# A two-layer decoder trunk: input projection dealt into a latent block of 328 columns and two groups' values as 512, gate with features on partitions, and x, w_in and the vectors laid out ahead

## The chip, the cores and the metric

The kernel runs on one core of a Trainium2 chip. The metric is the device time in microseconds (us) of one execution, as the median of several runs. The profile is one further execution, recorded by the hardware profiler.

## What is computed

All arithmetic is float32. `x` is 256 tokens by 1024 features, and there are two layers. Of the reference, what matters here:

```python
cond = silu(c)
for l in range(2):
    sh1, sc1, g1, sh2, sc2, g2 = split(cond @ w_ada[l] + b_ada[l], 6)
    h = rms_norm(x, norm1_gain[l]) * (1.0 + sc1) + sh1
    proj = h @ w_in[l]
    (qa, ka, va, qb, kb, vb, qc, kc, vc, fc, gc,
     qlat, kvlat, kidx, widx) = split(proj)   # nine of 256, then 4, 256, 128, 128, 64, 4
    ...                                       # four head groups: differential, block, forgetting, indexed
    o_c = forgetting_attention(qc, kc, vc, fc + f_bias[l]) * sigmoid(gc)
    q_lat, kv_lat = rms_norm(qlat), rms_norm(kvlat)
    ...                                       # q, k, v and the index scores of the fourth group from these
    x = x + g1 * (concat(o_a, o_b, o_c, o_d) @ w_out[l])
    h = rms_norm(x, norm2_gain[l]) * (1.0 + sc2) + sh2
    x = x + g2 * conv_glu_ffn(h, w_ffn_up[l], ffn_conv_w[l], ffn_conv_b[l], w_ffn_down[l])
return rms_norm(x, final_gain)
```

The input projection has 2888 columns: 9 x 256 for q, k and v of three groups (a, b, c), and 584 more: forget logits (4), gate (256), latents (128 + 128), index key (64), index weights (4).

## The kernel before

**Units.** Every large weight is used in units of 1 MB (128 partitions x 2048 floats). SP loads a unit into one of three buffers `raw`; ACT copies it, rounded, to `w_hi` (`split_hi`, L1437); DVE subtracts to get `w_lo` (`split_lo`, L1693); PE then computes three products per tile, hi x hi, hi x lo and lo x hi (`product3`, L979 to L981). Activations are split in the same way into `act_hi` (ACT, L1463) and `act_lo` (DVE, L1708). A buffer is loaded again when its `split_lo` three units back is done; `w_hi` is written again when PE has used that unit.

**The twelve units of the input projection** are `IN_UNITS`: unit 0 has the last 72 columns (index key, index weights and the rest of the latents) with features on partitions, which PE then transposes back (`narrow`, L1224); unit 1 has 256 and unit 2 the first 256 of the 584 columns (forget logits and nearly all of the gate); units 3 to 11 are q, k, v of the three groups, 256 columns each. For a unit PE goes over eight tiles of 128 input features (k) and two halves, which makes 48 matmuls of 256 moving columns (24 for unit 0). In q and k units the weights stand still and the 256 tokens move, so that features come out on partitions; in the others the activations stand still and the weight columns move, so that tokens come out on partitions. PE writes units alternately to PSUM banks 0 and 1, and may write a bank again when ACT has copied the unit before out of it (`evac`, L1513 to L1519, counted by the semaphore `in_read`).

**The gate** comes out with tokens on partitions, goes through a tanh on ACT and a scaling on DVE in the step `forget` (L1547, L1842), and is transposed in the middle of the attention (`gate_turn`: four PE transposes at L1339, one ACT copy at L1601), because the third group's output has features on partitions.

**Order of work.** `layer_schedule(l)` writes one list of steps; each engine goes through the list and issues its own part of every step, in that order. After the first units come the latents (norm, transposes L1231 and L1236, up-projections L1247 and L1251), the index scores (L1262), the forget sums, and then `maps()`, called thirteen times. Each call issues the scores of two heads on PE (L1188, L1190), the bias and minimum on DVE (L1889, L1891), the exponentials on ACT (L1578), and the transposes of earlier probabilities (L1299); halves of the remaining units stand between the calls and fill PE while DVE and ACT work. The step `choose` (top 64 of the index scores, L1863, L1864) is spread over DVE between them.

**Setup, before layer 0.** SP issues c, x, then `w_ada` units ("direct", 1 MB each, eight of them for the first shift and scale) mixed with the vectors as rows and the first units of `w_in`. PE transposes x (16 matmuls, L1124) and DVE copies it to `xT` (L1769); PE transposes the vectors too (L1114). PE multiplies the eight units with `cond` (L992, 16 matmuls each, two records to one matmul), two of them giving one quarter of shift and scale, and waits with dummy products (`keep_busy`, L1137). A quarter goes to `mod` through a transpose and an add on DVE (L1736, L1738). Shift (units 0 to 3) is loaded before scale (units 4 to 7) in each half:

```python
SETUP_COLUMNS = (0, SETUP_ADA // 2, 2, SETUP_ADA // 2 + 2)   # pairs: shift, scale, shift, scale
```

Of the kernel before, what the change touches and what calls it, by code (L numbers as in the profile page):

```python
# [22 lines left out]
P = 128  # L23
# [9 lines left out]
UC = 256  # L33
# [7 lines left out]
IN_COLS = C_FC + HEADS + GROUP + 2 * P + HEAD + HEADS  # L41
TAIL = IN_COLS - C_FC
T_GC, T_LAT = HEADS, HEADS + GROUP
T_KIDX = T_LAT + 2 * P
# [43 lines left out]
V_BADA, V_N1, V_N2, V_CB = 0, 48, 56, 64  # L88
V_W0, V_W1 = 128, 128 + 2 * FT
V_W2 = 256  # L90
VROWS = [64 + 2 * FT, 4 * FT, 2 * FT]
# [49 lines left out]
SETUP_COLUMNS = (0, SETUP_ADA // 2, 2, SETUP_ADA // 2 + 2)  # L141
# [25 lines left out]
def layer_schedule(l):  # L167
# [61 lines left out]
    if l == 0:  # L229
        s += [("unit", 0, 4, KT), ("evac", 0), ("split_hi", 3), ("unit", 1, 4, KT), ("evac", 1), ("split_lo", 3),  # L230
              ("unit", 2, 0, 4), ("narrow", 0), ("unit", 2, 4, KT), ("evac", 2), ("latents_norm", 0),
              ("split_hi", 4), ("split_lo", 4), ("unit", 3, 0, KT), ("evac", 3), ("latents", 0), ("lambda", 0),
              ("forget", 0), ("split_hi", 5), ("split_lo", 5)]
    else:
        for k in range(KT):
            s += [("unit", 0, k, k + 1), ("unit", 1, k, k + 1)]
        s += [("evac", 0), ("evac", 1), ("narrow", 0)]
        s += [("split_hi", 3), ("latents_norm", 0), ("split_lo", 3), ("unit", 2, 0, 4)]
# [8 lines left out]
    def first_half(i):  # L247
        s.append(("unit", i, 0, KT // 2))

    def second_half(i):  # L250
        s.extend([("unit", i, KT // 2, KT), ("evac", i)])
# [58 lines left out]
    s.append(("gate_turn", 0))  # L310
# [43 lines left out]
def trunk(nc, x, c, ada_units, b_ada, norm1_gain, w_in, f_bias, diff_lambda, diff_subln_gain, w_dq_up,  # L354
          w_didx_q, w_dkv_up, w_out, t5_table, norm2_gain, w_ffn_up, ffn_conv_w, ffn_conv_b,
          w_ffn_down, final_gain, buckets, out):
# [6 lines left out]
    with ExitStack() as ctx:  # L363
# [3 lines left out]
        def sem(name):  # L367
# [17 lines left out]
        tail = sb("tail", [P, TT, TAIL])  # L385
# [5 lines left out]
        vec = sb("vec", [P, DEPTH, 384])  # L391
# [29 lines left out]
        c_rows = sb("c_rows", [KT, P])  # L421
# [13 lines left out]
        narrow = work[0:NARROW, 768:768 + SEQ]  # L435
# [10 lines left out]
        gate_c = tail[:, :, T_GC:T_GC + GROUP]  # L446

        x_tok = heads_out[:, :, :, :].rearrange("p g t n -> p (g t n)").rearrange("p (t n) -> p t n", t=TT)
        rows_in = v_sb[:, 0:3, :, :].rearrange("p g t n -> p (g t n)")[:, 0:DEPTH * 384].rearrange(
            "p (l r n) -> p l r n", l=DEPTH, r=3)  # L450
# [15 lines left out]
        rows_sem = [sem("rows_early"), sem("rows_late")]  # L466
# [5 lines left out]
        c_turned = sem("c_turned")  # L472
        table_in = sem("table_in")
        diag_up = sem("diag_up")
        vec_turned = sem("vec_turned")
        x_turned = sem("x_turned")
# [32 lines left out]
        narrow_turned = sem("narrow_turned")  # L509
        narrow_read = sem("narrow_read")  # L510
# [29 lines left out]
        gate_turned = sem("gate_turned")  # L540
# [7 lines left out]
        gate_exp = sem("gate_exp")  # L548
# [29 lines left out]
        def vector_rows(l, t):  # L578

            return VROWS[t]  # L580

# [14 lines left out]
        def unit_bank(l, i):  # L596
            if (l, i) == (0, 2):
                return bank[2]
            return bank[i % 2 if i < NI else i - NI]
# [11 lines left out]
        def unit_width(i):  # L611
            return IN_UNITS[i][2] if i < NI else UC

# [28 lines left out]

        def unit_shape(i):

            return KT * unit_width(i)

# [28 lines left out]
        for st, i in [e[:2] for e in schedules[0]]:  # L675
            if st == "probs":
                turn_order.append(("probs", i))
            elif st == "turn" and i not in SIDE:
                turn_order += [("turn", i, 0)]
            elif st == "gate_turn":  # L680
                turn_order.append(("gate_turn", 0))
# [1405 lines left out]
```

## Time and profile before

| | |
|---|---|
| median of three runs | 727.2 us (727.04 to 727.21) |
| the profiled execution, its own time | 725.33 us |
| span of its profile | 723.6 us |
| PE busy | 699.5 us of the span |
| DVE, ACT, POOL busy | 504.2, 398.1, 121.9 us |
| read from HBM | 156.81 MB |

The span runs from the first to the last instruction; the execution's own time is 1.7 us longer. Matmuls overlap in the pipeline, so the duration of one is longer than its distance from the next, and an engine counted as busy can hide short waits. Stretches of the run: setup to about 38 us, layer 0's attention to about 160, its MLP to about 375, then the same for layer 1.

### The profile page before, as it was taken

Reading aid. Unit: us, or ns where it says so; the run is one execution under the profiler, and the core shown is the slowest. Engines: PE = TensorE matmul, PEld = TensorE weight load, DVE = VectorE, ACT = ScalarE, POOL = GpSimd, SP = SyncE. Lnnn points to the kernel's source line nnn. Section 1 sums busy time; section 2 is a strip of 40 time slices with the busy share of each in tenths; the row PEclk is TensorE's granted clock in tenths of the full one; section 3 lists DMA queues with packets and bytes.
Section 4 is the critical chain, followed back from the end, with each engine's and each line's share of the span. In section 5 each row is a group of like instructions: output and inputs, shape, how many; then the busy total and the mean of one; then the engine's idle time right before and its main releaser. Section 6 shows DMA issues by size and latency. Waiting matters only on the chain.

```text
span 723.6 us, 15426 instructions
## 1 busy us (share of the span) xinstructions
PE 699.5 (97%) x6461; PEld 660.3 (91%) x6461; DVE 504.2 (70%) x905; ACT 398.1 (55%) x644; POOL 121.9 (17%) x96
## 2 busy tenths in 40 slices
PE   6999999999999999999999999979999999999995
PEld 5898989899999999999999998869999999999993
DVE  2464788736888879887757568973687666666666
ACT  3258756735756464646445775573475555544552
POOL 2001003004044635363010010210400000000002
PEclk9999999999999999999999999999999999999998
DMA  9989998465386767687744875556526567555511
GB/s 320 382 221 249 395 341 323 178 234 175 118 291 233 260 207 256 210 291 254 286 131 137 299 265 191 187 221 234 175 83 215 164 211 249 187 175 175 183 50 58
DMA packets 98151, 159.43 MB, mean 220 GB/s; under 512 B 6035, under 2 KB 85028, under 8 KB 91940
## 3 DMA queue, kind: packets, MB, share of 16 engines
q1 hardware_dynamic: 98084, 158.46, 63.9%
q8 instruction: 51, 0.84, 0.5%
q14 instruction: 16, 0.13, 0.1%
HBM read 156.81 MB, written 1.64 MB: 219 GB/s over the span
## 4 chain that ended last, share of the span: by engine, by line
PE 78%; DVE 9%; ACT 6%; issue 3%; DMA 2%; SPq 1%; POOL 0%; DVEq 0%; POOLq 0%; ACTq 0%
PE bank L979 23%; PE bank L980 22%; PE bank L981 22%; PE bank L992 3%; DVE w_lo L1693 2%; ACT work L1578 2%; DMA direct<-in_w_ada 2%; DVE score L1864 1%; ACT w_hi L1437 1%; DVE top L1863 1%; PE bank L1025 1%; PE bank L1299 1%; SPq L747 1%; PE bank L1330 1%; DVE work L1889 1%
## 5 line engine op out<-in xcount | busy, mean ns | idle before, releaser
L1693 DVE TENSOR_TENSOR w_lo<-raw,w_hi 128x2048 fp32r<-128x2048 f32 (+1 forms) x97 | 238.4, 2458 | 95.2 <-ACT w_hi L1437 95.0
L979 PE MATMUL bank<-act_hi,w_hi 128*128 128x256 f32 (+1 forms) x1024 | 293.1, 286 | 0.3 <-DVE act_lo L1708 0.2
L980 PE MATMUL bank<-act_lo,w_hi 128*128 128x256 f32 (+1 forms) x1024 | 289.6, 283 | 0.0
L981 PE MATMUL bank<-act_hi,w_lo 128*128 128x256 f32 (+1 forms) x1024 | 289.6, 283 | 0.0
L1437 ACT ACTIVATE w_hi<-raw 128x2048 fp32r<-128x2048 f32 (+1 forms) x97 | 183.0, 1888 | 135.3 <-PE bank L981 133.2
L979 PEld LDWEIGHTS bank<-act_hi,w_hi 128*128 128x128 f32 (+1 forms) x1024 | 195.5, 191 | 4.3 <-issue 3.1
L980 PEld LDWEIGHTS bank<-act_lo,w_hi 128*128 128x128 f32 (+1 forms) x1024 | 195.6, 191 | 0.4
L981 PEld LDWEIGHTS bank<-act_hi,w_lo 128*128 128x128 f32 (+1 forms) x1024 | 195.5, 191 | 0.0
L1985 DVE SCALAR_TENSOR_TENSOR work<-bank,vec,work 128x254 f32<-128x254 f32 (+1 forms) x176 | 76.5, 476 | 11.2 <-ACT work L1637 9.6
L979 PE MATMUL bank<-mlp_hi,w_hi 128*128 128x256 f32 x192 | 54.7, 285 | 0.0
L980 PE MATMUL bank<-mlp_lo,w_hi 128*128 128x256 f32 x192 | 54.3, 283 | 0.0
L981 PE MATMUL bank<-mlp_hi,w_lo 128*128 128x256 f32 x192 | 54.3, 283 | 0.0
L1578 ACT ACTIVATE work<-work,low 128x128 f32<-128x128 f32 x80 | 35.6, 446 | 33.5 <-DVE low L1889 33.2
L1637 ACT ACTIVATE work<-bank,vec 128x256 f32<-128x256 f32 x88 | 44.3, 553 | 17.5 <-PE bank L981 17.4
L979 PE MATMUL bank<-w_hi,act_hi 128*128 128x256 f32 (+1 forms) x168 | 49.5, 294 | 0.1
L980 PE MATMUL bank<-w_lo,act_hi 128*128 128x256 f32 (+1 forms) x168 | 48.3, 288 | 0.0
L981 PE MATMUL bank<-w_hi,act_lo 128*128 128x256 f32 (+1 forms) x168 | 48.3, 287 | 0.0
L881 POOL TENSOR_TENSOR direct<-direct 128x1024 f32<-128x1024 f32 (+1 forms) x16 | 42.5, 2657 | 24.7 <-ACT direct L1455 23.8
L992 PE MATMUL bank<-direct,cond 128*32 128x128 f32 x1280 | 41.1, 277 | 0.6 <-DMA direct<-in_w_ada 0.6
L992 PEld LDWEIGHTS bank<-direct,cond 128*32 128x32 f32 x1280 | 33.7, 111 | 4.0 <-issue 1.0
L979 PEld LDWEIGHTS bank<-mlp_hi,w_hi 128*128 128x128 f32 x192 | 36.8, 192 | 0.3 <-issue 0.3
L980 PEld LDWEIGHTS bank<-mlp_lo,w_hi 128*128 128x128 f32 x192 | 36.8, 192 | 0.0
(214 smaller groups left out, 949.0 us busy)
## 6 DMA issues: line engine op xcount, KB each, us to landing
direct<-in_w_ada SPq DMA_DIRECT2D x48, 1024.0 KB, 8.9
raw<-in_w_ffn_up SPq DMA_DIRECT2D x44, 1024.0 KB, 5.2
raw<-in_w_in SPq DMA_DIRECT2D x22, 1024.0 KB, 6.7
raw<-in_w_ffn_down SPq DMA_DIRECT2D x22, 1024.0 KB, 4.9
raw<-in_w_out SPq DMA_DIRECT2D x8, 1024.0 KB, 4.9
bias<-toeplitz SPq DMA_DIRECT2D x4, 384.0 KB, 11.3
heads_out<-in_x SPq DMA_DIRECT2D x1, 1024.0 KB, 5.0
out<-heads_out SPq DMA_DIRECT2D x4, 256.0 KB, 2.2
```

The costliest lines, as they stand in the source:

```text
L747: sp.dma_start(dst, src).then_inc(raw_in[n % RAW], 16)
L881: nc.gpsimd.tensor_tensor(w[:, 0:m], w[:, 0:m], w[:, m:2 * m], ALU.add).then_inc(ada_added, 1)
L979: pe.matmul(dst, lh, rh, start=first, stop=False, skip_group_check=check)
L980: pe.matmul(dst, lh, rl, start=False, stop=False, skip_group_check=check)
L981: return pe.matmul(dst, ll, rh, start=False, stop=last, skip_group_check=check)
L992: mm = pe.matmul(pair_bank(l, u)[32 * g:32 * g + 32, 0:P], cond[:, 4 * half + k, :], w[:, k, g, :], start=(half == 0 and k == 0), stop=(ha ...
L1025: mm = pe.matmul(means[:, t, :], wide[:, k, t * P:(t + 1) * P], mean_w[:, 0:1].to_broadcast([P, MEAN_COLS]), start=(k == early_tiles(n) an ...
L1437: nc.scalar.activation(w_hi[n % RAW][:, 0:KT * width], raw[n % RAW][:, 0:KT * width], ACT.Copy).then_inc(hi_done, 1)
L1578: nc.scalar.activation(part, part, ACT.Exp, bias=low[:, i % 3, t:t + 1], scale=-1.0, accum_out=rsum[:, sum_slot(i)[0], t, sum_slot(i)[1]:s ...
L1637: nc.scalar.activation(conv[:, which, f, :], bank[which][:, f * SEQ:(f + 1) * SEQ], ACT.Identity, scale=vec[:, l, V_W2 + ch:V_W2 + ch + 1] ...
L1693: nc.vector.tensor_tensor(w_lo[n % RAW][:, s], raw[n % RAW][:, s], w_hi[n % RAW][:, s].bitcast(F32), ALU.subtract).then_inc(lo_done, 1)
L1985: ins = nc.vector.scalar_tensor_tensor(dst, bank[which][:, f * SEQ:(f + 1) * SEQ - lag], vec[:, l, tap + ch:tap + ch + 1], dst, ALU.mult, ...
```

## The change

The 584 columns are dealt anew. A latent block of 328 columns (latents, index key, index weights, forget logits) has tokens on partitions and takes banks 0 and 1, one for each half of the tokens. It comes in two units: tiles 0 to 5 (128 x 1968 floats) and tiles 6 and 7 (128 x 656). The 256 gate columns become a unit of their own with features on partitions, the eleventh, copied out through the tanh into `gate_T`; `gate_turn` and `narrow` go. The values of groups a and b become one block of 512 columns, again in two units of four tiles each, and banks 0 and 1 hold one half of the tokens each; both are copied out after the second unit. The host lays out `w_in`, `x`, `c` and the vectors so that every partition reads one contiguous run. PE's transposes of x, c and the vectors, and DVE's copies, go. In the setup scale is loaded before shift, and the loads and products are in another order.

```diff
-IN_UNITS = [("tail", 512, TAIL - 512), ("tail", 256, 256), ("tail", 0, 256)]
-NARROW = TAIL - 512
-IN_UNITS += [(what, g, UC) for g in range(3) for what in "qkv"]
+IN_UNITS = [("lat", 0, LAT, 0, 6), ("lat", 0, LAT, 6, KT), ("q", 0, UC, 0, KT), ("k", 0, UC, 0, KT),
+            ("vv", 0, 2 * UC, 0, KT // 2), ("vv", 0, 2 * UC, KT // 2, KT), ("q", 1, UC, 0, KT), ("k", 1, UC, 0, KT),
+            ("q", 2, UC, 0, KT), ("k", 2, UC, 0, KT), ("gate", 2, UC, 0, KT), ("v", 2, UC, 0, KT)]
+READ_BY = {("k", 0): 4, ("k", 1): 8, ("k", 2): 10, ("v", 0): 6, ("v", 1): 6, ("v", 2): 12}
...
-SETUP_COLUMNS = (0, SETUP_ADA // 2, 2, SETUP_ADA // 2 + 2)
+SETUP_COLUMNS = (SETUP_ADA // 2, 0, SETUP_ADA // 2 + 2, 2)
...
+            s.append(("tokens", i, 1))
+            if i == 5:
+                s.extend([("evac", 4), ("evac", 5)])
...
-                    src = w_in[l].rearrange("(k p) n -> p k n", p=P)[:, :, c0:c0 + width]
-                    dst = dst[:, 0:KT * width].rearrange("p (k n) -> p k n", k=KT)
+                    src = in_units[l, i, :, 0:unit_cols(i)]
+                    dst = dst[:, 0:unit_cols(i)]
...
+                for k, t in order:
+                    if wait_act is not None:
+                        pe.wait_ge(act_lo_ready, wait_act + k + 1)
+                    s = slice(t * P, (t + 1) * P)
+                    mm = product3(bank[t][:, 0:cols], (act_hi[:, k, s], act_lo[:, k, s]),
+                                  (wh[:, k - first, :], wl[:, k - first, :]), k == 0, k == KT - 1)
+                    if k == KT - 1 and t == 0:
+                        mm.then_inc(tokens_half, 1)
...
+                    elif st == "tokens":
+
+                        pe.wait_ge(in_read, NI * l + (4 if e[2] else 1))
+                        first = IN_UNITS[i][3]
+                        mm = wide_product(l, i, [(k, e[2]) for k in range(first, first + KT // 2)])
...
+                        if i in (0, 4):
+                            act.wait_ge(tokens_half, 2 * l + (2 if i else 1))
+                        else:
+                            act.wait_ge(unit_used, unit_no(l, i) + 1)
...
+                        elif kind == "vv":
+                            nc.scalar.activation(v_sb[:, 0:2, i - 4, :], bank[i - 4][:, :].rearrange("p (g n) -> p g n", g=2),
+                                                 ACT.Copy).then_inc(in_read, 1)
+                        elif kind == "gate":
+                            nc.scalar.activation(gate_T[:, :, :], src, ACT.Tanh, scale=0.5).then_inc(in_read, 1)
...
+            take_mod(0, 6)
+            first_low(4, 6)
+            split_lo(1, unit_cols(1))
+            first_low(6, KT)
+            front_part(1)
```

In layer 1 unit 2 (now q of group a) is written to bank 7, in layer 0 to bank 2 as unit 2 was before. The first call of `maps()` still stands between the two halves of unit 5.

**SP, the loads of the setup** (in_w_ada: the eight units; raw: the units of `w_in`; the four rows after the first two ada units before are the vectors as rows). Before:

```order
L774 DMA heads_out<-in_x 128x2x1024
L727 DMA direct<-in_w_ada 128x2048 x2
L717 DMA v_sb<-in_b_ada 48x2x128
L717 DMA v_sb<-in_norm_gain 8x2x128 x2
L717 DMA v_sb<-in_ffn_conv_b 44x2x128
L727 DMA direct<-in_w_ada 128x2048
L747 DMA raw<-in_w_in 128x8x72
L747 DMA raw<-in_w_in 128x8x256
L727 DMA direct<-in_w_ada 128x2048 x5
```

And now:

```order
L758 DMA xT<-in_x 128x2048
L708 DMA direct<-in_w_ada 128x2048 x2
L761 DMA vec<-in_vectors 128x480
L708 DMA direct<-in_w_ada 128x2048
L726 DMA raw<-in_w_in 128x1968
L708 DMA direct<-in_w_ada 128x2048
L765 DMA tab<-in_t_table 32x12
L766 DMA own_bias<-in_buckets 33x384
L708 DMA direct<-in_w_ada 128x2048 x2
L755 DMA raw<-in_w_in 128x1024
L708 DMA direct<-in_w_ada 128x2048 x2
L726 DMA raw<-in_w_in 128x656
```

The second unit of `w_in` stood ahead of the last five ada units; now the first one, larger, stands ahead of five, and half of unit 2 ahead of the last two.

**PE, the start of the setup**, before and then now:

```order
L1120 MATMUL bank<-ident,c_rows 128x8
L1124 MATMUL bank<-ident,heads_out 128x128 x16
L992 MATMUL bank<-direct,cond 32x128 x16
L1025 MATMUL bank<-mean_w,work 128x32 x10
L992 MATMUL bank<-direct,cond 32x128 x16
L1048 MATMUL bank<-ident,root 128x128 x2
L1114 MATMUL bank<-ident,v_sb 128x108 x2
L992 MATMUL bank<-direct,cond 32x128 x16
L1137 MATMUL bank<-ident 128x128 x20
```

```order
L1114 MATMUL bank<-ident 128x128 x13
L971 MATMUL bank<-direct,cond 32x128 x16
L1004 MATMUL bank<-mean_w,work 128x32 x10
L971 MATMUL bank<-direct,cond 32x128 x16
L1027 MATMUL bank<-ident,root 128x128 x2
L971 MATMUL bank<-direct,cond 32x128 x16
L1114 MATMUL bank<-ident 128x128 x24
L1127 MATMUL bank<-own_bias,tab 12x384
L971 MATMUL bank<-direct,cond 32x128 x32
```

The transposes are gone, dummy products stand in their place, and the table product (L1127) has moved ahead of the fourth ada unit.

**ACT, around the first `maps()`** (work,rsum<-work,low are the exponentials, v_sb<-bank the copy of values out of PSUM), with what each row waits for. Before:

```order
L1578 ACTIVATE work,rsum<-work,low 128x128 [waits low_ready]
L1578 ACTIVATE work,rsum<-work,low 128x256 [waits low_ready]
L1517 ACTIVATE v_sb<-bank 128x512 [waits unit_used]
L1437 ACTIVATE w_hi<-raw 128x2048 [waits unit_used,raw_in2]
L1578 ACTIVATE work,rsum<-work,low 128x128 [waits low_ready]
```

And now:

```order
L1540 ACTIVATE work,rsum<-work,low 128x128 [waits low_ready]
L1540 ACTIVATE work,rsum<-work,low 128x256 [waits low_ready]
L1476 ACTIVATE v_sb<-bank 128x2x256 [waits tokens_half]
L1476 ACTIVATE v_sb<-bank 128x2x256 [waits unit_used]
L1400 ACTIVATE w_hi<-raw 128x2048 [waits unit_used,raw_in2]
L1540 ACTIVATE work,rsum<-work,low 128x128 [waits low_ready]
```

Before, the copy of unit 4 stood ahead of the exponentials; now both copies of values stand behind them, and PE's next unit needs the first (it writes bank 0).

## Rows read from the trace of the kernel before

**Rows 1.** The page: the span; busy time and share of each engine.

```profile
span 723.6 us, 15426 instructions
...
PE 699.5 (97%) x6461; PEld 660.3 (91%) x6461; DVE 504.2 (70%) x905; ACT 398.1 (55%) x644; POOL 121.9 (17%) x96
```

**Rows 2.** PE waits, layer 0: line, released by, us in total, times, longest.

```profile
PE bank L1188 <- ACT qkT L1519: 0.7, 2, 0.6
PE bank L1299 <- DVE work L1925: 0.7, 1, 0.7
```

**Rows 3.** The same view, layer 1.

```profile
PE bank L1188 <- ACT qkT L1519: 2.2, 2, 1.7
PE bank L1330 <- DVE work L1900: 0.9, 1, 0.9
...
PE bank L1349 <- DVE work L1900: 0.6, 1, 0.6
```

**Rows 4.** Timeline of PE, equal matmuls in a row: start us, us (256 columns).

```profile
300.05 0.28 PE L980 MATMUL bank<-act_lo,w_hi 128*128 128x256 f32 x1
...
308.45 0.28 PE L981 MATMUL bank<-act_hi,w_lo 128*128 128x256 f32 x1
```

**Rows 5.** The same view, matmuls of 512 columns.

```profile
602.20 0.39 PE L980 MATMUL bank<-w_lo,mlp_hi 128*128 128x512 f32 x1
...
606.51 0.39 PE L981 MATMUL bank<-w_hi,mlp_lo 128*128 128x512 f32 x1
```

**Rows 6.** Windows: stretch, length, busy us of each engine, PEclk, DMA share, GB/s.

```profile
0.00:10.00 10.00, 3.93 (x21) 3.53 (x25) 2.14 (x4) 3.14 (x7) 2.37 (x15) 1.00 0.77 294
10.00:20.00 10.00, 9.97 (x151) 9.05 (x151) 2.09 (x5) 3.58 (x7) 2.13 (x3) 1.00 1.08 365
20.00:30.00 10.00, 9.18 (x144) 8.16 (x146) 6.35 (x12) 2.60 (x5) 0.00 (x0) 1.00 1.01 420
```

**Rows 7.** Timeline of PE: setup, latents, first index product, transposes of the gate.

```profile
22.12 1.08 PE L992 MATMUL bank<-direct,cond 128*32 128x128 f32 x32 [0.62 <-DMA direct<-in_w_ada]
...
25.83 0.31 PE L979 MATMUL bank<-act_hi,w_hi 128*72 128x256 f32 x1 [0.21 <-DVE act_lo L1708]
...
58.08 2.76 PE L1247 MATMUL bank<-heads_out,direct 128*128 128x256 f32 x12
...
65.21 0.50 PE L1262 MATMUL bank<-kiT,qiT 64*128 64x128 f32 x4 [0.65 <-ACT v_sb L1542]
...
119.71 0.60 PE L1339 MATMUL bank<-ident,tail 128*128 128x128 f32 x4
```

**Rows 8.** ACT groups, by form: busy us, mean ns.

```profile
L1437 ACT ACTIVATE w_hi<-raw 128x2048 fp32r<-128x2048 f32 x95 | 181.6, 1913 | 135.3 <-PE bank L981 133.2 <-DMA raw<-in_w_in 2.0
...
L1463 ACT ACTIVATE act_hi<-work,mod 128x256 fp32r<-128x256 f32 x32 | 15.7, 507 | 33.8 <-DVE work L1712 33.8
...
L1480 ACT ACTIVATE w_hi<-raw 128x1024 fp32r<-128x1024 f32 x1 | 1.0, 1042 | 0.0
```

**Rows 9.** DVE groups, by form.

```profile
L1693 DVE TENSOR_TENSOR w_lo<-raw,w_hi 128x2048 fp32r<-128x2048 f32 x95 | 236.9, 2493 | 95.1 <-ACT w_hi L1437 95.0
...
L1708 DVE SCALAR_TENSOR_TENSOR act_lo<-work,mod,act_hi 128x256 fp32r<-128x256 f32 x32 | 15.3, 479 | 1.7 <-ACT act_hi L1463 1.7
```

**Rows 10.** Timeline of PE, around the first maps() of layer 0.

```profile
73.48 0.49 PE L1188 MATMUL bank<-qkT 32*128 32x128 f32 x4
...
74.34 0.39 PE L979 MATMUL bank<-w_hi,act_hi 128*128 128x256 f32 x1
```

**Rows 11.** Timeline of ACT, the same stretch.

```profile
79.22 0.57 ACT L1517 ACTIVATE v_sb<-bank 128x512 f32<-128x512 f32 x1
```

**Rows 12.** Timeline of PE, layer 1, end of unit 1 and start of unit 2.

```profile
390.15 0.36 PE L979 MATMUL bank<-w_hi,act_hi 128*128 128x256 f32 x1
```

**Rows 13.** Timeline of DVE, the same stretch.

```profile
387.71 2.29 DVE L1693 TENSOR_TENSOR w_lo<-raw,w_hi 128x2048 fp32r<-128x2048 f32 x1 [1.32 <-ACT w_hi L1437]
```

**Rows 14.** Windows of layer 1, two stretches between calls of maps(), columns as in Rows 6.

```profile
450.00:460.00 10.00, 10.00 (x104) 9.47 (x107) 9.66 (x36) 6.44 (x18) 1.35 (x2) 1.00 0.33 107
470.00:480.00 10.00, 6.70 (x59) 5.47 (x59) 7.39 (x24) 6.73 (x22) 3.60 (x5) 1.00 0.70 262
```

More of the change, by code:

```diff
@@ L85 @@
 SCALE = [HALF ** -0.5, HEAD ** -0.5, HEAD ** -0.5, HEAD ** -0.5]
[L88 to L91, printed above, removed]
+V_BADA, V_N1, V_N2 = 0, 48, 56
+V_CB, V_W0, V_W1, V_W2 = [64 + 2 * FT * i for i in range(4)]
+V_COLS = 64 + 8 * FT
 def bucket_rows():
@@ L596, in unit_bank @@
         def unit_bank(l, i):
-            if (l, i) == (0, 2):
-                return bank[2]
+            if i == 2:
+                return bank[7 if l else 2]
             return bank[i % 2 if i < NI else i - NI]
@@ L1071, in unit_product @@
                     pe.wait_ge(lo_done, n + 1)
[L1072 to L1082 removed]
+                wh = w_hi[n % RAW][:, :].rearrange("p (k n) -> p k n", k=KT)
+                wl = w_lo[n % RAW][:, :].rearrange("p (k n) -> p k n", k=KT)
+                token_rows = i < NI and IN_UNITS[i][0] == "v"
                 out = NI <= i < NI + NO
@@ L1098, in unit_product, with wide_product, latent_unit @@
                 return mm
+            def wide_product(l, i, order, wait_act=None):
+                n = unit_no(l, i)
+                _, _, cols, first, end = IN_UNITS[i]
+                pe.wait_ge(lo_done, n + 1)
+                wh = w_hi[n % RAW][:, 0:unit_cols(i)].rearrange("p (k n) -> p k n", n=cols)
+                wl = w_lo[n % RAW][:, 0:unit_cols(i)].rearrange("p (k n) -> p k n", n=cols)
+                for k, t in order:
+                    if wait_act is not None:
+                        pe.wait_ge(act_lo_ready, wait_act + k + 1)
+                    s = slice(t * P, (t + 1) * P)
[3 more added lines that the diff above has]
+                        mm.then_inc(tokens_half, 1)
+                return mm
+            def latent_unit(l, i, k0, k1):
+                if l == 0 and i == 1:
+                    order = [(k, t) for t in range(TT) for k in range(k0, k1)]
+                else:
+                    order = [(k, t) for k in range(k0, k1) for t in range(TT)]
+                return wide_product(l, i, order, KT * 2 * l)
             def last_out_unit(l):
@@ L1491, in _ @@
+            act.wait_ge(vec_in, 16)
             for l in range(DEPTH):
@@ L2067, in ada_layout, with in_layout, vector_layout @@
     return units
+def in_layout(w_in):
+    tiles = w_in.reshape(DEPTH, KT, P, IN_COLS)
+    units = np.zeros((DEPTH, NI, P, KT * UC), np.float32)
+    for i, (kind, g, cols, first, end) in enumerate(IN_UNITS):
+        if kind == "lat":
+            take = list(range(C_LAT, IN_COLS)) + list(range(C_FC, C_GC))
+        elif kind == "gate":
+            take = list(range(C_GC, C_LAT))
+        else:
+            groups = (0, 1) if kind == "vv" else (g,)
+            take = [3 * GROUP * j + GROUP * "qkv".index(kind[0]) + n for j in groups for n in range(GROUP)]
+        part = tiles[:, first:end][:, :, :, take].transpose(0, 2, 1, 3)
+        units[:, i, :, 0:cols * (end - first)] = part.reshape(DEPTH, P, -1)
+    return units
+def vector_layout(v):
+    rows = [v["b_ada"], v["norm1_gain"], v["norm2_gain"], v["ffn_conv_b"]] + [v["ffn_conv_w"][:, t] for t in range(3)]
+    cols = np.concatenate([r.reshape(DEPTH, -1, P) for r in rows], axis=1)
+    return np.ascontiguousarray(cols.transpose(2, 0, 1))
 def kernel(**inputs):
```

388 lines of the change are left out of this document (157 added, 231 removed).

## The prediction

> **What bounds the kernel now.** I read the page first: PE is busy for 699.5 of 723.6 us, the others for 504 at most [rows 1]. So PE's list of work sets the time nearly everywhere, and PE's waits are the next view. They show little: in layer 0 after the setup 0.7 us for a copy on ACT and 0.7 for a mix on DVE, in layer 1 some more, the longest 1.7 [rows 2, 3]. Busy overstates PE, though, because records overlap; so the cost of a matmul comes from the distance between starts. From 300.05 to 308.45 there are 70 steps of 256 columns, 0.120 us each [rows 4]; from 602.20 to 606.51 19 steps of 512 columns, 0.227 us each [rows 5]. The 256 further columns cost 0.107 us, which is 2.4 GHz, the upper level (PEclk 1.00 [rows 6]), and about 0.013 us is paid per matmul. A matmul of 328 columns is then 0.120 + 72/256 x 0.107 = 0.150 us. The setup is another stage: there PE is filled with dummy products, and what it waits for is the fourth ada unit, a DMA that lets it go at 22.12 [rows 7], with the DMA engines at a share of 1.0 [rows 6].
>
> **PE work of the units.** Tail and gate took 24 + 48 + 48 matmuls of 0.120, 14.4 us per layer; now 48 of 0.150 and 48 of 0.120, 13.0 us. Values of a and b took 96 of 0.120, 11.5 us; now 48 of 0.227, 10.9 us. The gate's four transposes (0.60 us [rows 7]) go, and the two narrow ones, some 0.3. On paper that is 1.4 + 0.6 + 0.6 + 0.3 = 2.9 us per layer. What of it comes out depends on the place.
>
> The page "TensorE: Matmul & The Clock Gate" of the Trainium skill, section "Back-to-back issue gap", gives about 131 ns for a matmul of 512 columns in a stream with weight loads; by it the values would cost 6.3 us a layer and the change would save some 9 us more over both. The trace has 227 ns for just that pattern, so the sum does not use it.
>
> **Setup of layer 0, the largest term.** The DMAs set the pace. Ahead of and with the fourth ada unit lay 6.7 MB (x, four ada units, vectors, w_in units of 0.3 and 1.05 MB); when it had landed, 2.94 + 3.65 + 0.89 = 7.5 MB had moved [rows 6], so 0.8 MB of later loads was under way. Now 11.3 MB lie up to the eighth ada unit; with the same 0.8 and 2.94 in the first 10 us, 9.2 MB are left. In the stretch from 20 to 30 us, nearly all ada units in long runs, 420 GB/s moved; from 10 to 20, with short rows of w_in and vectors among them, 365 [rows 6]. Everything is in long runs now, so I take 420: the eighth lands at 31.8. At 365 it would be 35.1; both ends are kept.
> From there: its product 1.1 us [rows 7]; transpose and add on DVE, one act_hi (0.5 [rows 8]) and one act_lo (0.5 [rows 9]), 1.5 together; PE starts tile 4 at about 34.3. (Before, it took 3.7 us from 22.12 to 25.83 [rows 7], with scaling in between that is now done ahead.) ACT must then do two act_hi, the small split, two act_hi and the back half of unit 2 (1.04 [rows 8]), until 36.8; DVE follows to 38.0. PE ends the latents at 38.1 and unit 2 at 41.0. Unit 3's split stands on ACT behind the two copies of the latents: 38.8 to 40.7 (1.9 [rows 8]), then DVE 2.3 (the first 2.3 of [rows 13]) to 43.0. So PE waits 2 us here, a new wait. Then half of unit 3, six transposes, the other half (2.9 + 0.8 + 2.9), 12 matmuls of 512 (2.7), the up-projections (3.4, from 58.08 [rows 7] to where the units go on), another 12 (2.7): the first index product at 58.5, against 65.21 [rows 7]. That is **-6.7 us**, -3.4 with the slower DMAs, -7.2 if 420 GB/s hold from the first bytes on. The removed transposes of x (PE) and copies (DVE) lie ahead of the fourth ada unit and give nothing of their own. The gate unit is not in this stretch any more, and one and a half units of values stand for it later: the work left after the index point is 40.0 us of unit matmuls against 40.3, counted below.
>
> **Layer 0 after the index scores.** Half the values are 0.3 us cheaper, the gate's transposes give 0.6. Against that stands a new wait. Unit 6 (q of b) writes bank 0, and that bank now holds half the values until ACT has copied them; the copy stands behind the four exponentials of the first maps(). Before, they ended at 79.22, where unit 5's copy began [rows 11]; the first copy would now end at 79.8. PE, which had its first scores at 73.48 [rows 10], would be through both halves of the values at 76.9 on that clock: **+2.9 us**. Behind it on PE are unit 6, the next scores and everything else. ACT and DVE lose only the second copy (0.5), so PE's later waits for them shrink: both of [rows 2], 1.4 together, go. Net: -0.3 - 0.6 + 2.9 - 1.4 = **+0.6**, ends -0.9 (no wait) and +2.0 (nothing given back). The gate's tanh takes the place of a copy on ACT, and its scaling on DVE moves into the busy part; it reads and writes 512 columns, about the 0.5 us of an act_lo [rows 9], which I cost at nothing while PE is behind its chain, and at 0.5 in the range.
>
> **Layer 1.** The latents' 1.5 us is lost: PE would be through at 388.4, but unit 2 needs its w_lo, and DVE makes that from 387.71 to 390.00 [rows 13], a chain from act_hi that PE does not move. PE began unit 2 at 390.15 [rows 12] and will again; only the narrow transposes' rest, 0.1, comes out, and 0.3 of the values up to the index scores: -0.4. Later the same wait of 2.9 arises, but here PE has 2.2 + 0.9 + 0.6 of waits [rows 3] and more, where DVE is busy for 9.7 us of 10 at 450 to 460 and PE only for 6.7 at 470 to 480 [rows 14]. That is a chain over DVE and ACT, not PE, and it absorbs PE's lateness; it gains nothing either, so that the values' 0.3 and the gate's 0.6 vanish in it. One wait of 1.7 was for k of group c, now copied a unit earlier, but the exponentials behind it wait for a split on ACT. I take 0, ends -2.0 and +1.0. Layer 1: **-0.4**.
>
> **Sum.** -6.7 + 0.6 - 0.4 = -6.5: 725.3 becomes 718.8 for the profiled execution. The median of the runs lies 1.9 above that execution, so I predict **720.7 us**.
>
> **Rivals.**
> *All of the PE work comes out.* The values' copy is in time and layer 1's splits come earlier: -6.7 - 0.9 in layer 0 and -0.4 - 0.9 - 1.4 in layer 1, -10.3, 716.9 us. For: PE is the busiest. Against: the rows on unit 2 and on the exponentials. Chance 0.20.
> *The DMAs are no faster.* The w_in loads are the smaller part of the bytes, and more of them stand ahead of the eighth ada unit. At 365 GB/s the setup gives 3.4: 724.0 us. The skill's page "DMA: Bandwidth & Descriptors", section "Where 436 GB/s comes from", speaks for this side: it has loads from HBM bound at about 358 GB/s a core; by it the gain would be about 2 us. The 420 of the trace is against it. Chance 0.15.
> *DVE and ACT bound both layers' attention.* No wait is given back (+1.4), layer 1 ends 1.0 later than before instead of 0.4 earlier (+1.4), and the gate's scaling counts (+0.5): -3.2, 724.0 us. DVE's 9.7 of 10 is for it, PE's few waits in layer 0 against. Chance 0.12.
> *Slower: the clock falls in the setup.* PE has gaps of 1 to 2 us between the ada units from 23 to 43 us, where dummy products filled them before. If it fell to 1.2 GHz there, 48 matmuls of 328 and 48 of 256 columns cost 0.137 and 0.107 more each, 11.7 us, of which some 4 lie in the waits: +7.7, net +1.2, 728.4 us. It decides from where the clock stays down for over 17 us. Against: PEclk was 1.00 with PE busy for 3.9 of the first 10 us [rows 6]. Chance 0.04.
> *It does less than it says,* by several of these together: 725.5 to 727. Chance 0.04.
>
> **Numbers.** The forecast has 0.45. The range 716.0 to 724.6 takes in the first rival with slightly faster DMAs and the second and third; both ends lie beyond their prices. About 0.2% (1.5 us) is what a measurement of this kernel tells from no change. Faster by more: 0.91; within: 0.05; slower: 0.04.
>
> **What would show it.** Unit matmuls 0.150 apart for 328 columns and 0.227 for 512. Eighth ada product at about 32; tile 4 at 34; first index product at 58.5. A PE wait of some 2 us for w_lo of unit 3; one near 2.9 for the copy of values before unit 6 in both layers; one of 1.5 for w_lo of unit 2 in layer 1; the waits of [rows 2] gone. Wrong would be: 328 columns above 0.16, an eighth ada unit after 34, a PEclk below 1.00, or a first index product after 62.

## The result, and the profile after

The changed kernel takes 729.9 us (median of 13 runs, 727.5 to 731.8); the kernel before, run beside it, 727.2 (13 runs, 725.7 to 728.0). The ratio is 1.0035 with an interval of 1.0021 to 1.0048: slower by 0.35%. Forecast were 720.7 us and a range up to 724.6. The profiled execution took 730.36 us.

The page, to be read against [rows 1]: PE is busy for 4.2 us less, although time at a lower clock counts as busy too, and the span is 5.0 us longer.

```profile
span 728.6 us, 15023 instructions
...
PE 695.3 (95%) x6280; PEld 651.5 (89%) x6280; DVE 500.6 (69%) x901; ACT 394.3 (54%) x633; POOL 121.6 (17%) x96
```

PE's waits over the whole run of the changed kernel (line, released by, us in total, times, longest). [Rows 2, 3] had nothing longer than 1.7:

```profile
PE bank L958 <- ACT v_sb L1476: 7.0, 2, 4.4
PE bank L1312 <- ACT work L1550: 4.4, 2, 2.4
PE bank L958 <- DVE w_lo L1649: 3.3, 2, 1.9
```

The first is the copy of the values ahead of unit 6, the second the copy that the first `turn` hangs on (`turn` is the step that transposes a group's output), the third the two waits for w_lo that were forecast.

Where the time went shows when the same work is compared in the two timelines of PE. The kernel before (its first index product of layer 0 is in [rows 7], 65.21; these are the second pair of scores, the first `turn`, the same three in layer 1, and the last stretch of 512 columns):

```profile
80.28 0.49 PE L1188 MATMUL bank<-qkT 32*128 32x128 f32 x4
...
141.62 0.66 PE L1349 MATMUL bank<-ident,heads_out 128*128 128x128 f32 x4 [0.64 <-DVE work L1900]
...
411.68 0.49 PE L1262 MATMUL bank<-kiT,qiT 64*128 64x128 f32 x3
...
426.74 0.38 PE L1188 MATMUL bank<-qkT 32*128 32x128 f32 x2
...
487.56 0.33 PE L1349 MATMUL bank<-ident,heads_out 128*128 128x128 f32 x1 [0.65 <-DVE work L1900]
...
703.58 0.40 PE L979 MATMUL bank<-w_hi,mlp_hi 128*128 128x512 f32 x1
```

And the changed kernel, with the setup and the two long waits for values:

```profile
22.08 1.08 PE L971 MATMUL bank<-direct,cond 128*32 128x128 f32 x32
...
26.03 0.39 PE L958 MATMUL bank<-w_hi,act_hi 128*128 128x328 f32 x1 [1.21 <-DVE act_lo L1666]
...
33.63 1.08 PE L971 MATMUL bank<-direct,cond 128*32 128x128 f32 x32
...
36.63 0.39 PE L958 MATMUL bank<-w_hi,act_hi 128*128 128x328 f32 x1 [0.29 <-DVE act_lo L1666]
...
45.24 0.36 PE L958 MATMUL bank<-act_hi,w_hi 128*128 128x256 f32 x1 [1.88 <-DVE w_lo L1649]
...
60.73 0.50 PE L1234 MATMUL bank<-kiT,qiT 64*128 64x128 f32 x4
...
77.21 0.38 PE L958 MATMUL bank<-act_hi,w_hi 128*128 128x256 f32 x1 [4.42 <-ACT v_sb L1476]
...
81.77 0.38 PE L1155 MATMUL bank<-qkT 32*128 32x128 f32 x2
...
142.28 0.66 PE L1312 MATMUL bank<-ident,heads_out 128*128 128x128 f32 x4 [1.91 <-ACT work L1550]
...
392.21 0.38 PE L958 MATMUL bank<-act_hi,w_hi 128*128 128x256 f32 x1 [1.45 <-DVE w_lo L1649]
...
413.50 0.39 PE L1234 MATMUL bank<-kiT,qiT 64*128 64x128 f32 x2
...
428.14 0.38 PE L958 MATMUL bank<-act_hi,w_hi 128*128 128x256 f32 x1 [2.58 <-ACT v_sb L1476]
...
432.48 0.58 PE L1155 MATMUL bank<-qkT 32*128 32x128 f32 x2
...
492.61 0.44 PE L1312 MATMUL bank<-ident,heads_out 128*128 128x128 f32 x2 [2.44 <-ACT work L1550]
...
708.62 0.40 PE L958 MATMUL bank<-w_hi,mlp_hi 128*128 128x512 f32 x1
```

The changed kernel is 4.5 us ahead at the first index product, 1.5 behind at the second scores, level by 100 us (the waits of [rows 2] are given back), 0.7 behind at the first `turn`, 1.8 behind at layer 1's index product, 5.7 behind at its second scores, and 5.0 behind from its first `turn` to the end. So time is lost in three short places, each behind a wait: 6.0, 2.8 (from 0.6 ahead, where PE comes to the wait, to 2.1 behind) and 3.9 us. The waits, so far as they are longer than before, are 8.3 of these 12.7. The rest is in the windows of the changed kernel (columns as in [rows 6]; PEclk is the third from the right):

```profile
73.00:77.00 4.00, 0.00 (x0) 0.00 (x0) 2.94 (x11) 2.73 (x10) 0.00 (x0) 1.00 1.02 422
78.00:81.00 3.00, 3.00 (x16) 3.00 (x15) 1.53 (x1) 1.44 (x1) 0.00 (x0) 0.50 1.03 429
...
140.00:142.00 2.00, 0.37 (x4) 0.13 (x2) 2.00 (x9) 1.13 (x5) 0.00 (x0) 1.00 0.00 0
143.00:146.00 3.00, 3.00 (x16) 3.00 (x16) 1.26 (x4) 1.49 (x5) 0.00 (x0) 0.50 0.01 3
...
430.00:432.00 2.00, 2.00 (x11) 2.00 (x11) 1.59 (x1) 0.37 (x1) 0.00 (x0) 0.50 0.00 0
```

Behind the waits of 4.42, 1.91 and 2.58 us the granted clock is 0.50, the lower level of 1.2 GHz, for some 3 us, and the 24 matmuls that follow take 4.6, 4.5 and 4.3 us instead of 3.1 (before, from 70.42 to 73.48): about 1.4 us each time. The other executions have no profile, but their mean granted clock is on record: the fastest of the 13, 727.5 us, had 0.992, and the three slowest, 731.3 to 731.8 us, had 0.985. So most of the spread goes with the clock.

### The profile page after: what moved, and what is told of

Read it like the earlier page. It is cut to its first block, busy times and chain, and to the rows that moved or that the text cites. A ratio compares the mean times of both kernels' runs of the same rounds, so it can differ in the third digit from the quotient of the medians.

```text
span 728.6 us, 15023 instructions
## 1 busy us (share of the span) xinstructions
PE 695.3 (95%) x6280; PEld 651.5 (89%) x6280; DVE 500.6 (69%) x901; ACT 394.3 (54%) x633; POOL 121.6 (17%) x96
## 3 DMA queue, kind: packets, MB, share of 16 engines
HBM read 156.81 MB, written 1.64 MB: 217 GB/s over the span
## 4 chain that ended last, share of the span: by engine, by line
PE 76%; DVE 8%; ACT 6%; DMA 6%; issue 2%; SPq 1%; POOL 0%; DVEq 0%; POOLq 0%; ACTq 0%
PE bank L958 22%; PE bank L960 22%; PE bank L959 22%; PE bank L971 4%; ACT work L1540 2%; DVE w_lo L1649 2%; DMA own_bias<-in_buckets 2%; DMA raw<-in_w_in 2%; ACT w_hi L1400 2%; DMA toeplitz<-own_bias 1%; PE bank L1271 1%; PE bank L1004 1%; DVE score L1833 1%; SPq L747 1%; DVE top L1832 1%
## 5 line engine op out<-in xcount | busy, mean ns | idle before, releaser
L958 PE MATMUL bank<-act_hi,w_hi 128*128 128x256 f32 x1040 | 299.0, 287 | 10.4 <-ACT v_sb L1476 7.0
L960 PE MATMUL bank<-act_hi,w_lo 128*128 128x256 f32 x1040 | 295.5, 284 | 0.0
L959 PE MATMUL bank<-act_lo,w_hi 128*128 128x256 f32 x1040 | 295.4, 284 | 0.0
L958 PEld LDWEIGHTS bank<-act_hi,w_hi 128*128 128x128 f32 x1040 | 200.6, 193 | 15.0 <-ACT v_sb L1476 7.8
L959 PEld LDWEIGHTS bank<-act_lo,w_hi 128*128 128x128 f32 x1040 | 200.7, 193 | 0.4
L960 PEld LDWEIGHTS bank<-act_hi,w_lo 128*128 128x128 f32 x1040 | 200.6, 193 | 0.0
L860 POOL TENSOR_TENSOR direct<-direct 128x1024 f32<-128x1024 f32 (+1 forms) x16 | 44.4, 2777 | 25.2 <-ACT direct L1421 24.3
L958 PE MATMUL bank<-w_hi,act_hi 128*128 128x512 f32 (+2 forms) x104 | 36.9, 355 | 1.5 <-DVE act_lo L1666 1.5
L960 PEld LDWEIGHTS bank<-mlp_hi,w_lo 128*128 128x128 f32 x192 | 36.8, 192 | 0.0
L881 POOL TENSOR_TENSOR work<-work 128x256 f32<-128x256 f32 x11 | 19.1, 1739 | 103.2 <-ACT work L1409 102.4
```

The source lines that it names most:

```text
L860: nc.gpsimd.tensor_tensor(w[:, 0:m], w[:, 0:m], w[:, m:2 * m], ALU.add).then_inc(ada_added, 1)
L881: nc.gpsimd.tensor_tensor(wide[:, 0, :], wide[:, 0, :], wide[:, k, :], ALU.add).then_inc(pair_summed, 1)
L958: pe.matmul(dst, lh, rh, start=first, stop=False, skip_group_check=check)
L959: pe.matmul(dst, lh, rl, start=False, stop=False, skip_group_check=check)
L960: return pe.matmul(dst, ll, rh, start=False, stop=last, skip_group_check=check)
```

## Why the copies are late

The timeline of ACT in the changed kernel, ahead of the wait of 4.42 us:

```profile
70.33 1.92 ACT L1400 ACTIVATE w_hi<-raw 128x2048 fp32r<-128x2048 f32 x1 [1.74 <-DMA raw<-in_w_in]
72.26 1.28 ACT L1540 ACT_TABLE_LOAD   x1
74.81 0.40 ACT L1540 ACTIVATE work<-work,low 128x128 f32<-128x128 f32 x1 [1.27 <-DVE low L1858]
...
76.58 1.06 ACT L1476 ACTIVATE v_sb<-bank 128x512 f32<-128x512 f32 x2
```

ACT waits for the load of unit 7, splits it, then waits until DVE has made its w_lo (2.3 us) and the first minima, does the exponentials, and only then copies the values, which PE had finished at 72.80. The wait for the load differs from one execution to the next: 1.74 us here and 1.63 and 0.25 in two later versions with the same order at this place; with them PE's wait for the copy was 4.42, 4.32 and 2.92 us. So the profile shown has the longest of the three. At 79.22 the same copy began before [rows 11]: this chain gained 2.6 us of the setup's 4.5.

The first `turn` is another matter. Without `gate_turn` every later transposition has a number one lower, and the number's parity decides whether ACT or DVE copies it. PE's first `turn` needs the bank of the last transposition but one: before, DVE's copy from 141.01 to 141.56; now ACT's from 141.76 to 142.23, behind two exponentials.

## The experiments

Theory A: the order of the copies on ACT holds PE up. Theory C: so does the changed parity. Theory D: each such idle stretch costs 1.4 us more by the clock. Rival B: DVE and ACT bound the attention, and no order on them or on PE gives anything. All ratios are to the kernel before, run on the same chip.

**Both copies first**

```diff
     first_half(5)
+    s += [("evac", 4), ("evac", 5)]
     maps()
     second_half(5)          # no evac in it any more
```

> The changed kernel, with ACT's two copies of the first values (units 4 and 5) ahead of the four exponentials of the first maps instead of behind them. Theory A (PE's wait for these copies, 4.42 us in layer 0 and 2.58 in layer 1, and the half clock for some 3 us behind each, are what turned the gain into a loss): the copy ends at about 73.4 instead of 77.2, the wait of unit 6 shrinks to 0.6 in layer 0 and 0.5 in layer 1, the clock stays up behind both, and of the 8.8 us (3.8 + 2.1 + 2 x 1.45) at least half comes out: 721 to 726. Rival B (DVE and ACT bound both layers' attention, so PE's wait only moves to the next mix or transposition): the wait goes, others grow by as much, 728.5 to 731.

Measured: 726.8 us, ratio 0.9988 (0.9976 to 1.0000). Both waits for the copies are gone, and 3 us came out, less than theory A wanted. PE now waited 1.47 us for the first mix in each layer. In its profile the clock fell three times all the same: behind that wait in layer 0 and behind the first `turn` of both layers. ACT's second copy waited for PE until 72.3 and pushed the exponentials.

**The slot held**

```diff
+            elif st == "slot":
+                turn_order.append(("slot", 0))
...
+                        n = turn_no[("slot", 0)]
+                        wait_turned(pe, l, n - 2)
+                        pe.transpose(bank[4 + n % 2][:, 0:P], ident[:, :], ident[:, :]).then_inc(t_ready, 1)
```

> The changed kernel, with the removed gate step's place in the order of transpositions held by one small transposition, so that from there on ACT and DVE copy the same maps as in the kernel before. Theory C (with the step gone each later copy changed engine, and the one that the first turn waits for ends 0.66 us later): the wait before the first turn falls from 1.91 to about 1.2 in layer 0 and from 2.44 to about 0.7 in layer 1 (before: 0.65), the two waits of 0.8 for values in layer 1 shrink, the clock may stay up behind the turn of layer 0 (1.5 us): 726 to 728.5. Rival B (the chain over DVE and ACT sets the end whichever engine copies): 729 to 730.5.

Measured: 727.1 us, ratio 1.0008 (0.9993 to 1.0024). Within theory C's range. The first `turn` waits 1.12 and 1.86 us instead of 1.91 and 2.44; in layer 1 that is more than the 0.7 expected, since PE arrives there earlier. The two waits ahead of products with values in layer 1 did not shrink (0.72 and 0.86, now for DVE). The runs scatter from 724.6 to 730.3. The two shorter waits are 1.4 us; the mean granted clock of the runs is 0.990 against 0.988, so part of the 2.8 us is the clock.

**Both**

> Both edits, the copies of values first and the slot held. Theories A and C together: 718.5 to 722.5, below the kernel before by over 0.5%. Rival B: no better than the better of the two alone by more than 1 us.

Measured: 723.6 us, ratio 0.9950 (0.9938 to 0.9963). The two edits add up (3.1 + 2.8 against 6.3 us), and the kernel is faster than before; rival B in its strong form is out. The forecast of 718.5 to 722.5 was missed by 1 us: the wait of 1.5 us for the first mix stays.

**Idle stretches filled, too long**

```diff
+            def fill(bk, count):
+                for _ in range(count):
+                    pe.matmul(bk[:, 0:P], ident[:, :], ident[:, :], start=True, stop=True)
...
+                            if i == 5:
+                                pe.wait_ge(ck_ready, HEADS * (l + 1))
+                                fill(bank[4], (18, 33)[l == 0])
...
+                        if i == 0:
+                            pe.wait_ge(in_read, NI * l + 11)
+                            fill(bank[0], (19, 14)[l == 0])
```

> The changed kernel with its order as it is, but PE fills the two stretches with dummy products of 128 columns (0.117 us each): 33 and 18 of them ahead of unit 6's wait in layers 0 and 1, 14 and 19 ahead of the first turn. No wait is shorter; only idleness is. Theory D (the granted clock falls to half behind these idle stretches, at 78 to 81, 143 to 146 and 429.5 to 433 us, and each fall costs 1.4 us): clock 1.00 throughout, the 24 matmuls behind take 3.1 instead of 4.6 us, 725.5 to 727.5. Rival (the clock falls for another reason, or the time lost at half clock is covered by the chain over DVE and ACT): 729 to 730.5.

Measured: 732.0 us, ratio 1.0071 (1.0058 to 1.0084), outside both forecasts, by a mistake in the size. I had taken 0.117 us per record for one product; an fp32 product has two records. The timeline of this version:

```profile
72.13 7.53 PE L1113 MATMUL bank<-ident 128*128 128x128 f32 x66
79.42 0.36 PE L958 MATMUL bank<-act_hi,w_hi 128*128 128x256 f32 x1
```

PE was busy with dummies past the end of every wait. The clock was 0.997 over the profiled execution, so the half of the theory on the clock stands; its price needed another run.

**Idle stretches filled, sized to the waits** (17 and 9 products ahead of unit 6 in layers 0 and 1, 7 and 9 ahead of the first `turn`)

> The filling again, now within the waits: a dummy product of fp32 takes two passes, 0.234 us, so the first filling ran 3.1, 1.6, 1.4 and 2 us past the waits' ends. Now 17 and 9 products ahead of unit 6 (4.0 and 2.1 us against waits of 4.4 and 2.6) and 7 and 9 ahead of the first turn (1.6 and 2.1 against 1.9 and 2.4), the order otherwise that of the changed kernel. Theory D (half clock behind idle stretches costs 1.4 us each time, three times in the profiled run): clock 0.997 or more, 725.5 to 727.5. Rival: 729 to 730.5.

Measured: 725.3 us, ratio 0.9978 (0.9969 to 0.9987), 0.2 below the range expected by theory D. The windows of this version, over the three places:

```profile
70.00:80.00 10.00, 10.00 (x76) 9.32 (x78) 6.81 (x14) 6.41 (x13) 0.41 (x1) 1.00 1.01 420
...
140.00:150.00 10.00, 9.99 (x131) 9.08 (x131) 2.23 (x6) 6.08 (x12) 0.00 (x0) 1.00 0.44 163
...
420.00:430.00 10.00, 9.43 (x107) 8.29 (x109) 7.34 (x23) 6.16 (x16) 0.00 (x0) 1.00 0.48 174
```

Nothing in this version is computed earlier or ordered otherwise than in the changed kernel; PE only does useless work where it was idle, and 4.6 us come out, half of the 9.2 by which the forecast missed. Theory D is shown, and the time at half clock is not covered by any other chain. The mean granted clock of the runs rose from 0.988 to 0.995. The 4.6 us are rather too little: in this profile ACT did not wait for unit 7's load, and the 17 products ended at 76.45, about 1 us after the first copy of values.

**Unit 3's split ahead of the latents' copies**

```diff
-        s += [("unit", 0, 4, 6), ("unit", 1, 6, KT), ("evac", 0), ("evac", 1), ("split_hi", 3), ...
+        s += [("split_hi", 3), ("unit", 0, 4, 6), ("unit", 1, 6, KT), ("evac", 0), ("evac", 1), ("split_lo", 3), ...
```

> The changed kernel, with unit 3's split on ACT and DVE ahead of the two copies of the latents in layer 0. The wait of PE for w_lo of unit 3 (1.88 us) should go and the first index product come at about 59.0 instead of 60.7, if unit 3's weights have landed by 38.7. Theory E (the start of attention hangs on the loads and splits of units 6 and 7, not on PE): the wait for the copies of values grows by as much, and the time stays within 1 us of the changed kernel's 729.9. Rival (the setup is bound by PE, and its gain is carried on): 727.5 to 728.5.

Measured: 730.8 us, ratio 1.0052 (1.0038 to 1.0067): within 1 us of the changed kernel, as theory E had it, but only half tested, because the wait for w_lo of unit 3 fell just from 1.88 to 1.27. The wait for the copies did not grow as theory E says; it was 4.32.

**One copy first, slot held**

```diff
+    s.append(("evac", 4))
     maps()
     second_half(5)          # evac 5 behind it
```

> As the version with both copies first and the slot held (723.55), but only the first copy of values stands ahead of the exponentials of the first maps; the second, which waited on ACT for PE until 72.32 and pushed them to 74.23, stands behind them as in the changed kernel. Theory A: unit 6 is still not held up, the exponentials start at 73.4 or earlier, the wait for the first mix falls from 1.48 to below 1 in both layers: 722 to 723. Rival B: no difference, 723 to 724.

Measured: 721.9 us, ratio 0.9929 (0.9915 to 0.9944). PE ran on into unit 6 without a wait, the exponentials began at 73.21, and the wait for the first mix is 0.56 us in layer 0 and gone in layer 1. That is 0.1 below the range expected by theory A and 8.0 us below the changed kernel, from nothing but the place of one copy and one small transposition.

**Unit 7's split behind the first maps, and behind their mix too**

```diff
-    split(7)
     first_half(5)
     s.append(("evac", 4))
     maps()
+    split(7)
     second_half(5)
```

> The changed kernel with three edits: only the first copy of values (unit 4, the one whose bank unit 6 writes) ahead of the exponentials of the first maps, the slot held, and unit 7's split behind these exponentials, so that they need not wait for its load or for its 1.9 + 2.3 us. Theory E (loads and splits hold up the first maps): the exponentials start at about 71 instead of 74.2, PE's wait for the first mix (1.48 us with both copies first) goes, and the kernel is faster than the version with both copies first (723.55) by 1.5 to 3.5: 720 to 722. Rival B (from 80 us on DVE is the bound, 19 of 20 us busy at 100 to 120, so that an earlier first map gives nothing): 723 to 724.

Measured: 724.7 us, ratio 0.9961 (0.9950 to 0.9973), slower than the version above, against both forecasts. The timeline of DVE in this version shows why:

```profile
71.94 0.08 DVE L1873 DVE_READ_ACCUMULATOR2_ANT low<- 128x1 f32 x1
75.59 2.29 DVE L1662 TENSOR_TENSOR w_lo<-raw,w_hi 128x2048 fp32r<-128x2048 f32 x1 [3.56 <-ACT w_hi L1413]
77.79 0.16 DVE L1902 RECIPROCAL ratio<-rsum 128x2 f32<-128x2 f32 x1
```

The minima were indeed ready at 72.0 instead of the changed kernel's 75.7, but the mix, issued behind the w_lo, could start only at 77.79. PE waited 1.64 us for it, 1.63 in layer 1, and behind both waits this profile's clock fell (0.50 from 80 to 82 and from 428 to 430 us), as it did from 45 to 48 behind the wait for unit 3. The version above had one fall in its profile ahead of the last 6 us. Two falls more are as much as the 2.8 us between the two versions. So the split was put behind the mix as well:

> The version with one copy first and the slot held (721.90), with unit 7's split behind the first maps AND behind their mix, and unit 8's split behind it. In the run with the split between the maps and the mix the mix waited for 2.3 us of w_lo on DVE. Theory E: the exponentials start at 71.2, the mix follows at once, PE's waits for the first mixes (0.56, 0.36, 0.75) shrink: 720.5 to 721.5. Rival B (DVE is the bound from there; two w_lo in a row, 4.6 us, hold up the second pair of maps instead): 722 to 725.

Measured: 721.9 us, ratio 0.9935 (0.9917 to 0.9953), no better than with the split in its old place, and between the two forecasts. Here rival B holds in its weak form: once PE is not held up by the order, an earlier first map gives nothing that these runs can tell.

**When had the eighth ada unit landed?**

```diff
-            unit_product(0, 2, bank[2], None, 0, 2)
             ada_half(0, 6, 1, 4)
-            unit_product(0, 2, bank[2], None, 2, 4)
+            unit_product(0, 2, bank[2], None, 0, 4)
```

> The changed kernel, with the two quarter products of unit 2 behind the product of the eighth ada unit instead of one ahead of it and one behind. It tells when that unit had landed. Theory F (PE's own list held it up, 1.65 us of unit 2 ahead of it, and the DMA was in time as forecast, at 31.8): the product starts at about 32.0 without a wait. Rival G (the DMAs were as late as the product, 33.6): PE waits for the DMA until 33 or later. The time: within 1 us of the changed kernel's 729.9 by both, since ACT's splits of units 6 and 7 decide when the first maps start.

Measured: 729.2 us, ratio 1.0035 (1.0016 to 1.0054), the changed kernel's. Its timeline of PE:

```profile
32.46 1.08 PE L971 MATMUL bank<-direct,cond 128*32 128x128 f32 x32 [1.00 <-DMA direct<-in_w_ada]
```

The unit landed at about 32.5, between theory F (32.0, no wait) and rival G (33 or later). The changed kernel's own trace agrees: the load was issued at 23.22 and landed 9.4 us later, at 32.6, and PE used it at 33.63. So the load was 0.8 us later than forecast, and PE's list held the product up for another 1.0. Starting it earlier gave no time, since PE then had the other quarter product to do. The profile of this version also shows the scatter of the clock, with waits at the same places as in the changed kernel (2.92, 1.88, 2.58 and 2.44 us). Windows behind the first and the last of them:

```profile
75.00:79.00 4.00, 3.55 (x30) 3.42 (x32) 2.37 (x5) 2.69 (x3) 0.00 (x0) 1.00 1.01 422
...
487.00:491.00 4.00, 4.00 (x23) 4.00 (x23) 1.26 (x4) 1.52 (x5) 0.00 (x0) 0.59 0.02 4
```

Here the clock fell behind the last one alone, where the changed kernel's had stayed up, and not behind the other three. The execution took 725.5 us, against this version's median of 729.2 and the 730.4 of the changed kernel's profiled one. Of these 4.8 us two falls fewer are some 2.8, and a first wait shorter by 1.5 most of the rest.

**Dummy products in the version with one copy first** (4 and 7 ahead of the first `turn`; then also 7 ahead of unit 3 in layer 0 and 5 ahead of unit 2 in layer 1)

> The version with one copy first and the slot held (721.90), and 4 and 7 dummy products (0.9 and 1.6 us) ahead of the first turn, whose waits are 1.16 in layer 0 and 1.86 in layer 1. Theory D (its one fall, clock 0.83 at 480 to 490 us, costs 1.4 to 1.7 and follows this wait): clock 1.00 there, 720.0 to 721.0. Rival (no more to gain from the clock): 721.7 to 722.3.

> The version of the run before (one copy first, slot held, dummy products ahead of the first turn; 721.16), and 7 dummy products more ahead of unit 3 in layer 0 (1.6 us; its wait for w_lo is 1.9 to 2.1) and 5 ahead of unit 2 in layer 1 (1.2 us against 1.44). Theory D, for the setup: the clock fell behind the wait for unit 3 in that version's profile (0.72 at 44 to 50 us, the 24 matmuls took 4.6 us for 3.1), as it did in some of the other versions; with the wait filled it does not, 719.5 to 720.5, and the spread of the runs falls. Rival (no fall left that costs PE anything on the path, or the dummy products run over the waits' ends): 721.0 to 721.8.

Measured: 721.2 us, ratio 0.9920 (0.9904 to 0.9936), and 721.0 us, ratio 0.9915 (0.9895 to 0.9936). Windows of the first, then of the second version:

```profile
44.00:50.00 6.00, 5.12 (x31) 5.16 (x32) 4.40 (x10) 1.20 (x1) 0.00 (x0) 0.72 0.84 210
```

```profile
44.00:50.00 6.00, 5.78 (x49) 5.58 (x49) 4.21 (x10) 2.80 (x4) 0.00 (x0) 1.00 0.87 215
```

The fall in the setup, behind the wait of 2.1 us for unit 3, went where the wait was filled. The times of these two and of the version without dummies (721.9) have intervals that overlap, so no further gain is shown. Theory D expected at most 721.0 and 720.5; the first is between it and its rival, the second at the edge of the rival's range. The clock did stay at 1.00 behind the filled `turn` of both layers. The runs of the last one lie closer together, 720.3 to 721.2, but they are four. These are the fastest versions, 0.8% below the kernel before.

## Why the prediction was wrong

It forecast 6.5 us less, and 2.7 more came out. The mechanisms that it named are there; what failed are three steps: "PE starts tile 4 at about 34.3", which left out PE's own list; the price of PE's waits, put at their length with nothing for the clock behind them; and "it absorbs PE's lateness" in layer 1. A slip beside these: the gain of "about 2 us" in its second rival is 2.7 by its own sum.

**Prices of the matmuls: right.** In layer 1, 45 steps of 328 columns from 383.70 to 390.45 are 0.150 us each; between the index products of layer 0, 10 steps of 512 columns from 66.28 to 68.57 are 0.229 each.

**Setup, -6.7 forecast, -4.5 found.** The DMAs did nearly what was forecast: 417 GB/s from 20 to 30 us, the eighth unit there at 32.6 instead of 31.8. The step that failed is "PE starts tile 4 at about 34.3": it followed the DMA, then DVE and ACT, and never added up PE's own list. By that chain alone the load's 0.8 us would have made it about 35.1. From 26.03 on PE had 24 matmuls of 328 columns, three ada products and 24 matmuls of 256 columns to do, and came to tile 4 at 36.63, having waited 0.3 us in all that. Everything behind kept its distance, 2.2 us later than forecast: unit 3 at 45.24 (43.0), first index product at 60.73 (58.5). The wait of 2 us for w_lo of unit 3 was 1.88.

**Layer 0 after the index scores, +0.6 forecast, +6.6 found** (from 4.5 us ahead to 2.1 behind). The wait for the copies was forecast with its mechanism and place, and 2.9 us long; it was 4.42. The 2.9 were read on the old clock, as if ACT moved up with PE. PE came over 4 us earlier than on that clock, ACT's copy only 2.6, because of unit 7's load and split. Where the load was late by only 0.25, in the run on the eighth ada unit, the wait was 2.92, so that the size came out right there. The waits of [rows 2] were given back as forecast. What the sum lacked is the price of an idle PE beyond the idleness: about 1.4 us at half clock, twice in this stretch. The prediction looked for a fall of the clock in the setup alone, as its rival for "slower", and needed 17 us of it; here it came in spells of 3 us, behind waits that the prediction itself had forecast.

**The gate's transposes, -0.6 in layer 0.** PE got to the first `turn` 0.6 us earlier and waited 1.91 instead of 0.64 there. That removing the step would move the copies between ACT and DVE was not seen at all; the version with the slot held gives 2.8 us back, part of it by the clock.

**Layer 1, -0.4 forecast, +2.9 found.** The latents' gain was lost to w_lo of unit 2 (wait 1.45, forecast 1.5) and 0.2 to 0.3 came out up to the index product (2.06 us behind where unit 2 begins, 1.82 at the index product; forecast 0.4). The step that failed is "absorbs PE's lateness". From the index product to the second scores the kernel lost 3.9 us, 2.6 by the wait and 1.3 by the clock. Afterwards its waits add up to 5.2 us, as they had before; they moved from k of group c and the mixes to the first `turn` with its changed copy, and gave nothing back but 0.7.

**Sum.** Between the forecast and the median lie 9.2 us, and filling the waits takes 4.6 of them away. Not all of these were missing from the forecast. It had added 1.9 us because the median of the kernel before lies above its profiled execution, and that distance goes with the clock too: of the recorded executions of the kernel before, those with a mean granted clock of 0.996 or more took 725.2 to 726.8 us, and all but one of the others, at 0.992 to 0.995, took 726.5 to 728.3. So the profiled executions are the fairer comparison: 718.8 forecast, 725.1 with the waits filled and no fall in the setup or the attention, 730.4 with three falls there. Of the 6.3 us that are left without falls, 2.2 are the setup; the other 4 are the longer wait in layer 0, the one in layer 1 that was not absorbed, and the first `turn`. How these 4 are shared out is not settled by a run. The gain itself is there: with one copy moved and the slot held the changed kernel takes 721.9 us.

## What to carry to other kernels

A wait of an engine that sets the end is to be priced with what follows it: here each PE wait of 1.5 to 4.4 us could cost about 1.4 us more by the clock, and a run in which dummy products fill the waits tells that share at once. When a resource gets a new, wider use (a bank that now holds two units), look where its release stands in the order of the engine that frees it; and when a numbered step is taken out, look for everything that goes by the parity of the number. A time at which a DMA lands bounds the start of the work only after the engine's own list up to there has been added up.

## What was not expected of the hardware

PE's granted clock fell to half behind stretches in which PE did nothing for 1.5 to 4.4 us, for about 3 us each time. In the changed kernel PE had been busy without a wait for 27 us ahead of the 4.42, 39 us ahead of the 1.91 and 33 us ahead of the 2.58. It is not certain: behind the waits of 1.9, 2.4 and 2.6 us a fall came in one profile and none in another, with the same order of work in the attention. The profiled execution of the kernel before, whose waits in the attention are at most 1.7 us, showed no fall there. But it was one of the faster ones (725.33 us, clock 0.996); most other executions of the same kernel had 0.992 to 0.995 and took 1 to 3 us more. So short waits are not shown to be safe; where the clock was lower in those executions no profile shows.
